# Two-block model on one core: five more stages take the first product of a stage by kind of product

## What is computed

```python
def first_block(x, norm_g, ...):
    for layer in range(DEPTH):
        hf = _swiglu(_rms_norm(x, g[0]), ffn_w_gate[layer, 0], ffn_w_up[layer, 0], ffn_w_down[layer, 0])
        x = x + 0.5 * _rms_norm(hf, g[1])
        xn = _rms_norm(x, g[2])
        mix = _attn_mixer(xn, ...) if layer % 2 == 0 else _mlstm_mixer(xn, ...)
        x = x + _rms_norm(mix, g[3])
        hf = _swiglu(_rms_norm(x, g[4]), ffn_w_gate[layer, 1], ffn_w_up[layer, 1], ffn_w_down[layer, 1])
        x = x + 0.5 * _rms_norm(hf, g[5])

def second_block(x, ...):
    for l in range(DEPTH):
        h = rms_norm(x, norm_g[l])
        p = h @ w_in[l]
        ...
        x = x + merged @ w_o[l]
```

## Time and profile before

| | |
|---|---|
| median of 3 runs | 1579.9 us (1578.57 to 1579.92) |
| the profiled execution: its time | 1579.87 us |
| its span on the core | 1578.1 us |
| PE matmul busy | 1564.3 us, 99% |
| PE weight loads busy | 1296.5 us, 82% |
| DVE busy | 973.1 us, 62% |
| ACT busy | 810.4 us, 51% |
| chain that ended last | PE 94%, DVE 3%, ACT 2% |

### The profile page before, as it was taken

How to read it: one execution, slowest core, us unless ns; L and a number is a source line. 1 busy time by engine, 2 the same in 40 slices (tenths; PEclk the granted TensorE clock), 3 DMA queues, 4 the chain that set the end, 5 groups by cost and what they waited for, 6 DMA issues and landing times.

```text
span 1578.1 us, 19384 instructions
## 1 busy us (share of the span) xinstructions
PE 1564.3 (99%) x7499; PEld 1296.5 (82%) x7499; DVE 973.1 (62%) x1227; ACT 810.4 (51%) x1016; POOL 56.6 (4%) x99
## 2 busy tenths in 40 slices
PE   8999999999999999999999999999999999999999
PEld 6888888888888888888878888887888888788887
DVE  5555576674545645466677455568956665895664
ACT  5544455464444544356766444466365446636542
POOL 2000010000000000000000000011000000100000
PEclk9999999999999999999999999999999999999999
DMA  9654763256448553564436544664434456443443
GB/s 297 220 176 147 249 216 122 88 193 198 148 148 277 176 189 130 187 228 161 160 125 209 195 151 150 231 216 172 171 107 160 165 190 229 171 167 107 161 168 126
DMA packets 189125, 279.23 MB, mean 177 GB/s; under 512 B 8541, under 2 KB 102917, under 8 KB 189056
## 3 DMA queue, kind: packets, MB, share of 16 engines
q1 hardware_dynamic: 186784, 271.27, 49.7%
q0 software_dynamic: 2128, 6.97, 1.4%
q10 hardware_dynamic: 144, 0.03, 0.0%
HBM read 277.20 MB, written 1.06 MB: 176 GB/s over the span
## 4 chain that ended last, share of the span: by engine, by line
PE 94%; DVE 3%; ACT 2%; DMA 1%; issue 1%; SPq 0%; DVEq 0%
PE ACC L864 24%; PE ACC L865 24%; PE ACC L871 24%; PE TB L901 3%; PE ZB L1040 2%; PE ACC L1070 2%; PE ACC L1072 2%; PE ACC L1071 2%; PE ACC L1170 1%; PE ACC L792 1%; PE ACC L1172 1%; PE ACC L1171 1%; PE TB L889 1%; PE ACC L948 1%; PE ACC L947 1%; PE ACC L954 1%
## 5 line engine op out<-in xcount | busy, mean ns | idle before, releaser
L2105 DVE TENSOR_TENSOR WL<-RAW,WH 128x2048 fp32r<-128x2048 f32 (+2 forms) x256 | 508.3, 2027 | 238.0 <-ACT WH L1450 237.1
L864 PE MATMUL ACC<-WH,XH 128*128 128x512 f32 (+2 forms) x1272 | 495.9, 391 | 0.3 <-DVE XL L2134 0.2
L1450 ACT ACTIVATE WH<-RAW 128x2048 fp32r<-128x2048 f32 (+3 forms) x254 | 419.6, 1699 | 139.2 <-PE ACC L871 91.2
L865 PE MATMUL ACC<-WH,XL 128*128 128x512 f32 (+2 forms) x1272 | 488.7, 385 | 0.0
L871 PE MATMUL ACC<-WL,XH 128*128 128x512 f32 (+2 forms) x1272 | 334.7, 385 | 0.0
L864 PEld LDWEIGHTS ACC<-WH,XH 128*128 128x128 f32 x1272 | 239.1, 188 | 49.6 <-issue 2.0
L865 PEld LDWEIGHTS ACC<-WH,XL 128*128 128x128 f32 x1272 | 239.2, 188 | 45.2
L871 PEld LDWEIGHTS ACC<-WL,XH 128*128 128x128 f32 x1272 | 236.3, 188 | 47.9
L864 PE MATMUL ACC<-WH,HH 128*128 128x512 f32 x352 | 137.7, 391 | 0.0
L865 PE MATMUL ACC<-WH,HL 128*128 128x512 f32 x352 | 137.0, 389 | 0.0
L2240 DVE SCALAR_TENSOR_TENSOR ST<-ACC,RX,SIDE 128x256 f32<-128x256 f32 x88 | 41.8, 480 | 149.0 <-ACT SIDE L1549 147.5
(11 more groups left out here) (334 smaller groups left out, 1809.8 us busy)
## 6 DMA issues: line engine op xcount, KB each, us to landing
RAW<-w_in_in SPq DMA_DIRECT2D x66, 1024.0 KB, 6.8
RAW<-ffn_w_gate_in SPq DMA_DIRECT2D x42, 1024.0 KB, 5.2
RAW<-ffn_w_up_in SPq DMA_DIRECT2D x42, 1024.0 KB, 7.4
RAW<-ffn_w_down_in SPq DMA_DIRECT2D x32, 512.0 KB, 4.5
RAW<-ffn_w_down_in SPq DMA_DIRECT2D x16, 1024.0 KB, 6.1
RAW<-mlstm_w_in_in SPq DMA_DIRECT2D x16, 1024.0 KB, 6.9
RAW<-ffn_w_down_in SPq DMA_DIRECT2D x16, 768.0 KB, 6.1
RAW<-attn_w_in_in SPq DMA_DIRECT2D x12, 1024.0 KB, 7.1
```

The source lines that it names most:

```text
L864: nc.tensor.matmul(bank, lh, wh[:, i, :], start=first and i == 0, stop=False)
L865: nc.tensor.matmul(bank, ll, wh[:, i, :], start=False, stop=False)
L1450: nc.scalar.activation(WH[:, slot, lo:hi], RAW[:, slot, lo:hi], ACT.Copy).then_inc(hi_ready, 1)
L2105: nc.vector.tensor_tensor(WL[:, slot, lo:hi], RAW[:, slot, lo:hi], WH[:, slot, lo:hi].bitcast(F32), ALU.subtract).then_inc(lo_ready, 1)
```

## The change

The condition under which the first block goes through `by_kind` is widened from "the stage before is attn or mlstm" to "any stage but the first, if the block has 512 columns". It now holds in stages 1, 3, 4, 6 and 7 as well. The first blocks of all these have 512 columns.

```diff
-                    mixed_ahead = fresh is not None and stages[at.stage - 1][0] in ("attn", "mlstm")
+                    mixed_ahead = fresh is not None and at.stage > 0 and n == COLS
```

## The result

| | before | after |
|---|---|---|
| median | 1579.03 us (12 runs, 1578.26 to 1579.92) | 1583.46 us (12 runs, 1581.7 to 1585.35) |
| profiled execution: time, span | 1579.87, 1578.1 us | 1582.87, 1581.1 us |

The ratio is 1.0029 with a 95% interval of 1.0022 to 1.0037: 4.4 us slower. The two medians put the cost at 3.3 and 4.4 us, the two intervals together at 1.9 to 5.8. The forecast of +4.4 is the larger of the two medians.

The account below looks back on a forecast made before the run. PE, running end to end, was taken to bound the kernel; a turning 1.36 us later gives 1.36 - 0.1 + 0.4 + 2.7 = 4.4 us on 1579.87, so 1584.3 us, 0.28% slower, with a range of 1581.3 to 1586.0.

Parts of the forecast that it names:

- What bounds: Whole kernel: PE runs end to end, 99% busy; the change can act only through waits that go or come.
- Waits that go: Block starts and turnings of token tile 2: -0.1 us for stage 3, nothing elsewhere.
- asks that come earlier: First blocks: WL's second half needed after 12 matmuls, not 20, and XH 4 behind the turning; 0, at most 0.1 per stage.
- Stage 1, +1.36: Stage 1 (attn): the turning of ST, where PE waits for ACT already, moves by the whole 1.36 us; ends 0.9 and 1.6.
- the bias wait: Stage 1, bias table: PE waits 0.9 to 1.1 us for XL, inside the later turning of ST, not on top.
- Stage 4, +0.4: Stage 4 (mlstm): ACT takes the gates later, WL and then LF on DVE follow; +0.4 us, ends 0 and 1.0.
- Stages 6 and 7, +1.36 each: Mixers (mix2): load of c+3 leaves 1.36 us later, split, rotation and ST follow; 2.7 together, ends 0.9 and 2.1 each.
- the signs named: New trace: among others, PE's wait for ST in stage 7 up from 0.67 to about 2.0 us, about 1.3 in stage 6.
- The spread of the forecast: Forecast's own 1582.7 to 1585.4 us, given as stage 4 from 0 to 1 and stage 1 from 0.9 to 1.6.
- (a): Rival: chains have hidden room, only the bias wait shows, 0 to 1 us elsewhere; 1580.8 to 1582.5 us; 14%.
- (b): Rival: not slower; stage starts and turnings gain 0.85 us, ACT's chain has 1.36 us of room in four stages; 1579.0; 3%.
- (c): Rival: mixers' load of c+3 slowed by that of c+4, up to 0.7 us later again per stage; 1585.7 us; 12%.

Follow-up runs that it names:

- e4: The change with only the turning of token tile 2 put back to 14 matmuls behind the block's start: 1579.26 us, +0.2 over before.
- e1: The kernel before with the order by kind added in stage 1 (attn) only: 1580.61 us, +1.5 over before.
- e5: The change with stage 1's bias table moved 8 matmuls further, into token tile 2: 1582.71 us, +3.4 over before.
- e12: Second measurement of the change with the bias table 8 matmuls later, beside the change on one chip: 1583.81 us, ratio 1.0028.
- e8: The kernel before with the order by kind added in stages 3 (ffn) and 4 (mlstm) only: 1579.48 us, +0.4 over before.
- e7: The change with DVE rotating iq ahead of the split of chunk c+3: 1579.75 us, +0.5 over before.
- e10: The change with ACT making both halves of WH of chunk c+1 before squaring x in stages 6 and 7: 1580.75 us, +1.5 over before.
- e9: The change with token tile 2's turning at its old place and DVE rotating iq before the split of c+3: 1577.55 us, -1.7 against before.
- e3: The kernel before, old order of products, with token tile 2's turning behind 20 matmuls in all stages but stage 0: 1586.08 us, +6.8 over before.
- e11: The change itself measured again in another batch, unaltered: 1582.5 us, ratio 1.0022 against before.

## Why the prediction was right, and where it was not

**What bounds.** Right. PE's busy share did not change, and waits are the whole difference. The Trainium skill's rule (Perfetto Trace Analysis, "Identifying the Most-Contended Engine") read as 18% of room would have made the change free; weight loads are at 82% again, and every delay that reached PE came out in the time. PE stands at 83% where it waits for nothing, so in this kernel the measure does not end at 100%, and the 82% was no room.

**Waits that go, and asks that come earlier.** Right, at about 0. The turning of stage 1 took 203.47 - 202.68 = 0.79 us, where it was 202.68 - 201.73 = 0.95 before, and stage 3 came to -0.1. WL was never late in a first block, and `e4` shows the two together: +0.2 us.

**Stage 1, +1.36.** Measured +1.33 in the profile and +1.5 by `e1`. That the bias wait lies inside the later one was the step with a rival on it: the traces of `e5` and `e12` leave the distance from turning to turning where it was and have the idle time before L901 in place of L1056. Their medians are too unsteady to say it by themselves.

**Stage 4, +0.4.** Measured +0.27. It was the right place (L1224), and by `e8` (+0.4 us, 0.23 of it at L1224) stages 3 and 4 together are below what a measurement tells.

**Stages 6 and 7, +1.36 each.** The chain was right: `e7` cuts it at the rotation and `e10` at the load's start, and both take most of the mixers' loss away. The size was about right for stage 7 (+1.24) and off for stage 6 (+0.67). Of the signs named, the wait for ST in stage 7 came to 1.78 us for 2.0, and the one in stage 6 to 0.59 for 1.3. What was mis-sized is the step that the load, leaving 1.36 us later, also lands so much later. ACT and DVE in the changed kernel, stage 6:

```profile
1037.46 1.52 DVE L2105 TENSOR_TENSOR WL<-RAW,WH 128x1312 fp32r<-128x1312 f32 x1 [1.88 <-ACT WH L1450]
...
1046.47 3.72 ACT L1450 ACTIVATE WH<-RAW 128x2048 fp32r<-128x2048 f32 x2 [0.98 <-DMA RAW<-w_in_in]
```

WL was done at 1038.98 and ACT had the data at 1046.47, 7.5 us later. Before it was 1044.73 against the same WL row ending at 1036.56, 8.2 us. The load left late and was quicker. It is the same in the other traces: with the late turning and the order by kind in stage 6, this time was 7.5 to 7.7 us in five of six traces and 8.4 in the sixth (`e12`); with the early turning it was 8.0 to 8.3 in five of six (in the sixth, `e9`, the load had landed before ACT was free), and with the late turning in the old order (`e3`) 8.6. In `e11` and `e12` the waits of PE for ST in stage 6 differ by as much:

```profile
1055.89 1.09 PE L901 MATMUL TB<-CT,ST 128*128 128x128 f32 x8 [0.76 <-DVE ST L2574]
```

```profile
1057.18 1.09 PE L903 MATMUL TB<-CT,ST 128*128 128x128 f32 x8 [1.52 <-DVE ST L2576]
```

So stage 6 costs 0.7 to 1.6 us from one execution to another. With the 1.33 - 0.1 + 0.27 + 1.24 of the other stages the sum is 3.4 to 4.3 us.

**The number.** The forecast difference of 4.4 us equals the first measured one, and this is in part luck: the steps in the trace of the change add up to 3.4, and the second measurement has 3.3. The spread of the forecast, 1582.7 to 1585.4, does not follow from the terms named for it either. Stage 4 from 0 to 1 and stage 1 from 0.9 to 1.6 give 1583.4 to 1585.1, and the uncertain term was another, the load of stage 6.

**Rivals.** (a), room that the rows hide, fell by the traces: stages 1, 4 and 7 moved about as followed and stage 6 by half, 3.4 us in all, where (a) ends at 2.6. The times alone hardly exclude it, since the second measurement of the change, 1582.5 us, is the end of its range. (b) fell with it. (c), loads that slow each other, is spoken against: in the change the load of c+3 was not the slower one, although the next load followed it more closely: SP issued it 3.1 us behind (1039.01 and 1042.09), and 4.1 us behind before (1036.59 and 1040.70). The slowest, 9.1 us in `e10`, had the next load further behind (6.2 us) than in any other run, since DVE split chunk c+2 only from 1040.98. This agrees with the Trainium skill (DMA: Bandwidth & Descriptors, "Two DMAs through the same engine are not ordered"), by which descriptors of one queue start in order.

**Still open.** Why this load of stage 6 takes 7.5 us in one kernel and 8.2 or 9.1 in another. No run varied it alone. The trace of `e10` shows that there the delay lies at the end of the load. The DMA moves some 400 GB/s until 1043.8, and sinks to 48 GB/s in the slice at 1044.1, but ACT starts on the data only at 1046.24. These are the GB/s of 40 slices of 0.3 us from 1036 to 1048:

```profile
GB/s 0 0 0 0 0 0 0 82 55 164 335 375 403 416 410 410 403 416 444 382 375 403 362 375 389 423 260 48 157 130 137 341 389 403 423 403 403 410 423 403
```

So by far the most of the load had been moved 7 us after it left; whether a small rest or the signal of its end came late, this view does not tell.

## What to carry to other kernels

A transpose that PE does early feeds a chain on other engines, and moving it by six matmuls moves that chain, not PE. Before postponing one, follow what it releases, engine by engine, to the next place where PE asks for a result of the chain, and read there whether PE waits already. Where a chain ends in such a wait, look first at the queue of the engine at its end: work that needs nothing from the late input, as the rotation of iq, may stand behind it for no reason, and moving it was worth 1.6 us, more than any order of the matmuls that was tried here.

## What was not expected of the hardware

The load of chunk c+3 in stage 6, always of one size, through the same queue and with nothing ahead of it, took 7.5 (the change), 8.2 (before) and 9.1 us (`e10`) from the end of the subtraction that lets it leave to the start of ACT's work on the data. The same load in stage 7 took 8.6 to 9.0 us in every trace. A chain that PE waits for and that has a load in it may be what makes the time of a kernel less steady: the change ran from 1581.7 to 1585.35 us in its first measurement, where the kernel before ran within 1.7 us; with the chain cut (`e7`) the runs were within 1.7 us again (1578.9 to 1580.62). The second measurement of the change was within 1.5 us, however, so this is seen, not shown. The profiled executions of the change were at 1582.5 and 1582.87 us; what an execution near 1585 us waits for, no trace shows.
